# First output-projection tile fed tile by tile, and the second down unit made ready one block earlier

## The reference, cut to what matters

```python
merged = (jax.nn.sigmoid(ga) * (attn_o @ p["w_attn_br"])
          + jax.nn.sigmoid(gr) * (rwkv_o @ p["w_rwkv_br"]))
x = x + gate1[:, None, :] * (merged @ p["w_out"])
h2 = _modulate(_rmsnorm(x, p["norm2_g"]), shift2, scale2)
up = _dwconv3(h2 @ p["ffn_up"], p["ffn_conv"])
up_u, up_g = jnp.split(up, 2, axis=-1)
x = x + gate2[:, None, :] * ((jax.nn.silu(up_g) * up_u) @ p["ffn_down"])
```

## Time and profile before

| what | value |
|---|---|
| median of 3 runs | 1376.88 us (1375.66 to 1378.38) |
| the profiled execution's own time | 1380.84 us |
| its span, first to last instruction | 1379.1 us |
| PE busy in the span | 1294.0 us (94%) |
| DVE busy, ACT busy | 689.9 us (50%), 550.1 us (40%) |
| mean granted TensorE clock | 0.977 |

### The profile page before, as it was taken

One profiled execution on the slowest core, in us unless ns is written; L12 is line 12 of the kernel. 1 busy time (PEld: TensorE's weight loads), 2 busy tenths in 40 slices (PEclk: granted clock), 3 DMA queues, 4 the chain that ended last, 5 costly groups with the idle time before them and its releaser, 6 DMA issues.

```text
span 1379.1 us, 31730 instructions
## 1 busy us (share of the span) xinstructions
PE 1294.0 (94%) x13903; PEld 1196.7 (87%) x13903; DVE 689.9 (50%) x1036; ACT 550.1 (40%) x864; POOL 42.1 (3%) x103
## 2 busy tenths in 40 slices
PE   4899999998999769899999899899999999899996
PEld 1899999997999545499989788799999999899995
DVE  3437642642544676565556412654545545434544
ACT  4645534422233477533342121733334333233433
POOL 0100011000010000010000000000000000000000
PEclk9999999999999998999999999999999999999998
DMA  9322365315000200011017574021221211022222
GB/s 389 143 71 102 110 271 180 105 45 209 8 5 4 92 1 1 0 53 34 8 41 259 225 294 177 31 88 65 64 88 61 91 61 46 23 66 71 69 76 92
DMA packets 24027, 131.70 MB, mean 96 GB/s; under 512 B 2896, under 2 KB 3664, under 8 KB 15344
## 3 DMA queue, kind: packets, MB, share of 16 engines
q1 hardware_dynamic: 19104, 103.98, 21.5%
q0 software_dynamic: 4816, 26.11, 5.0%
HBM read 111.74 MB, written 18.34 MB: 94 GB/s over the span
## 4 chain that ended last, share of the span: by engine, by line
PE 60%; DVE 3%; ACT 2%; issue 1%; DVEq 0%; ACTq 0%
PE ps L712 30%; PE ps L1206 11%; PE ps L882 2%; PE ps L870 2%; PE ps L1093 1%; PE ps L850 1%; PE ps L737 1%; PE ps L756 1%; PE ps L1069 1%; PE ps L999 1%; PE ps L747 1%; DVE nmax L1972 1%; PE ps L1070 1%; PE ps L862 1%; PE ps L1040 1%
## 5 line engine op out<-in xcount | busy, mean ns | idle before, releaser
L712 PE MATMUL ps<-h2lo,whi 128*128 128x322 f32 x672 | 154.5, 311 | 0.7 <-ACT facc L1308 0.7
L712 PE MATMUL ps<-h2hi,wlo 128*128 128x322 f32 x672 | 155.0, 312 | 0.0
L712 PE MATMUL ps<-h2hi,whi 128*128 128x322 f32 x672 | 154.0, 310 | 0.0
L1662 DVE TENSOR_TENSOR wlo<-raw,whi 128x2048 fp32r<-128x2048 f32 x47 | 107.5, 2288 | 70.4 <-ACT whi L1269 70.4
L712 PE MATMUL ps<-hlo,whi 128*128 128x322 f32 x544 | 127.9, 316 | 1.0 <-ACT qkv L1334 1.0
L712 PE MATMUL ps<-hhi,wlo 128*128 128x322 f32 x544 | 125.4, 312 | 0.0
L712 PE MATMUL ps<-hhi,whi 128*128 128x322 f32 x544 | 124.7, 310 | 0.0
L712 PEld LDWEIGHTS ps<-h2hi,whi 128*128 128x128 f32 x672 | 114.2, 190 | 0.0
L712 PEld LDWEIGHTS ps<-h2lo,whi 128*128 128x128 f32 x672 | 113.0, 189 | 0.9 <-DVE wlo L1662 0.9
L712 PEld LDWEIGHTS ps<-h2hi,wlo 128*128 128x128 f32 x672 | 113.6, 189 | 0.0
L1709 DVE SCALAR_TENSOR_TENSOR facc<-fraw,par,facc 128x642 f32<-128x642 f32 x44 | 39.0, 887 | 138.7 <-ACT facc L1308 138.7
(11 more groups left out here) (339 smaller groups left out, 2596.7 us busy)
## 6 DMA issues: line engine op xcount, KB each, us to landing
raw<-in_wblk SPq DMA_DIRECT2D x48, 1024.0 KB, 4.9
adl<-in_wada SPq DMA_DIRECT2D x8, 2048.0 KB, 7.9
raw<-in_wdn SPq DMA_DIRECT2D x44, 256.0 KB, 2.6
adaw<-in_wada SPq DMA_DIRECT2D x4, 2048.0 KB, 20.7
gate_scratch<-gout POOLq DMA_DIRECT2D x16, 322.0 KB, 2.5
gld<-gate_scratch POOLq DMA_DIRECT2D x8, 644.0 KB, 4.6
attention_inputs_used<-attention_scratch SPq DMA_DIRECT2D x1, 5056.0 KB, 15.5
u_scratch<-uout POOLq DMA_DIRECT2D x12, 320.0 KB, 2.4
```

The source lines that it names most:

```text
L712: mm = pe.matmul(o, w, v, start=first, stop=last and w is hi and x is xh[n])
L1662: TT(wlo[s][:, :], raw[s][:, :], whi[s][:, :].bitcast(F32), ALU.subtract).then_inc(lo_done, 1)
```

## The change

The first output tile leaves `dense_block` and becomes `out_first`: it waits for `m_lo` one tile at a time, and `ada_late(4)` moves to just before its last tile. The other seven output tiles stay as they were. For the second down unit, the high and low data go to new tiles laid over the unused part of `raw[0]`, and its weights to columns 512 to 1023 of `whi[0]` and `wlo[0]`; so its ACT part and its DVE part move to between the last two up blocks, behind those of unit 0. ACT's wait for the last `af` tile stays, ahead of the loop over the other units.

```diff
+    spot[0] = raw_at + 4 * 512
+    dhi_second, dlo_second = (sb(name, [P, TP - 2], F32R) for name in ("dhi_second", "dlo_second"))
...
-        pe.wait_ge(tile_evac, 2 * BLK_OUT + 2)
-        ada_late(4)
-        pe.wait_ge(m_lo, KD)
+        def out_first():
+
+            pe.wait_ge(lo_done, BLK_OUT + 1)
+            pe.wait_ge(hi_done, BLK_OUT + 1)
+            pe.wait_ge(tile_evac, 2 * BLK_OUT + 1)
+            for k in range(KD):
+                if k == KD - 1:
+                    pe.wait_ge(tile_evac, 2 * BLK_OUT + 2)
+                    ada_late(4)
+                pe.wait_ge(m_lo, k + 1)
+                hi, lo = (w[BLK_OUT % 2][:, k * 256:k * 256 + P] for w in (whi, wlo))
+                for q, (w, x) in enumerate(((hi, mlo[k]), (lo, mhi[k]), (hi, mhi[k]))):
+                    for o, v in zip(out_halves(0), halves(x)):
+                        mm = pe.matmul(o, w, v, start=k == 0 and q == 0, stop=k == KD - 1 and q == 2)
+            mm.then_inc(tile_done, 1)
...
-        for b in range(BLK_OUT, BLK_UP):
+        out_first()
+        between_out(0)
+        pe.wait_ge(tile_evac, 2 * BLK_OUT + 2)
+        dense_tile(BLK_OUT % 2, 1, range(KD), mhi, mlo, out_halves(2), 256).then_inc(tile_done, 1)
+        between_out(1)
+        for b in range(BLK_OUT + 1, BLK_UP):
...
         def down_unit(n, s, k, again=False):
+
+            second = k == 1 and n == 1
             pe.wait_ge(d_hi, n + 1)
             pe.wait_ge(d_lo, n + 1)
+            xh, xl = (dhi_second, dlo_second) if second else (dhi[s], dlo[s])
             for f in (2, 3, 0, 1) if k == 0 and not again else range(4):
-                hi, lo = whi[s][:, f * P:f * P + P], wlo[s][:, f * P:f * P + P]
+                at = (4 + f if second else f) * P
+                hi, lo = (w[0 if second else s][:, at:at + P] for w in (whi, wlo))
...
-                for q, (w, x) in enumerate(((hi, dlo[s]), (lo, dhi[s]), (hi, dhi[s]))):
+                for q, (w, x) in enumerate(((hi, xl), (lo, xh), (hi, xh))):
...
-            ac.activation(whi[s][:, 0:512], raw[s][:, 0:512], ACT.Copy)
-            ac.activation(dhi[s][:, :], af[:, k, :], ACT.Copy).then_inc(d_hi, 1)
+            second = first and s == 1
+            ac.activation(whi[0][:, 512:1024] if second else whi[s][:, 0:512], raw[s][:, 0:512], ACT.Copy)
+            ac.activation((dhi_second if second else dhi[s])[:, :], af[:, k, :], ACT.Copy).then_inc(d_hi, 1)

         up_block(NBLK - 2, FF - 2, 0, False, False)
-        ac.wait_ge(act_done, 1)
+        ac.wait_ge(act_done, 2)
         ac.wait_ge(tile_done, 2 * NBLK - 2)
         down_hi(0, 0, 0, True)
+        down_hi(1, 1, 1, True)
         up_block(NBLK - 1, FF - 1, 1, False, False)
-
         ac.wait_ge(act_done, FF)
-        ac.wait_ge(tile_done, 2 * NBLK)
-        down_hi(1, 1, 1, True)
...
-        def down_lo(n, s, k):
+        def down_lo(n, s, k, second=False):
             dv.wait_ge(d_hi, n + 1)
-            TT(wlo[s][:, 0:512], raw[s][:, 0:512], whi[s][:, 0:512].bitcast(F32), ALU.subtract)
-            TT(dlo[s][:, :], af[:, k, :], dhi[s][:, :].bitcast(F32), ALU.subtract).then_inc(d_lo, 1)
+            wh, wl = (w[0][:, 512:1024] if second else w[s][:, 0:512] for w in (whi, wlo))
+            xh, xl = (dhi_second, dlo_second) if second else (dhi[s], dlo[s])
+            TT(wl, raw[s][:, 0:512], wh.bitcast(F32), ALU.subtract)
+            TT(xl[:, :], af[:, k, :], xh[:, :].bitcast(F32), ALU.subtract).then_inc(d_lo, 1)

         up_block(NBLK - 2, FF - 2, 0, False)
         down_lo(0, 0, 0)
+        down_lo(1, 1, 1, second=True)
         up_block(NBLK - 1, FF - 1, 1, False)
-        down_lo(1, 1, 1)
```

More of the change, by code:

```diff
@@ L383, in build @@
     yrs = sb("yrs", [P, TP])
+    spot[0] = raw_at + 4 * 512
+    dhi_second, dlo_second = (sb(name, [P, TP - 2], F32R) for name in ("dhi_second", "dlo_second"))
+    assert spot[0] <= raw_at + 4 * WEL
     spot[0] = af_at
```

## The result

The changed kernel takes 1370.68 us (median of 8 runs, 1368.39 to 1372.69); the kernel before, run beside it, 1378.47 (8 runs, 1375.66 to 1383.63). The ratio is 0.9941, with a 95% interval from 0.9926 to 0.9957: by it 8.1 us faster, between 5.9 and 10.2 (the medians differ by 7.8). A second round beside other kernels gave 0.9938 [0.9918, 0.9958]. The forecast was 11.5 us and a time of 1365.4; it had the direction and the two places right, and the size wrong. Part of the distance is the base: the forecast stood on the first three runs of the kernel before, 1376.88.

A forecast was written before the change was run, and what follows sets the result against it. PE was taken as the bound, busy 94% of the span, with idle and half clock at two places. Gains of 5.5 us (output projection) and 6.0 us (down units), 11.5 us off 1376.88, gave 1365.4 us; range 1362.5 to 1370.

The forecast's parts named there:

- Output tile 0 without a pause: At the output projection, PE goes straight on from the branch products; tile 1 starts 5.5 us sooner.
- The wait for tile 6 of `mlo`: In output tile 0, PE waits about 0.3 us for the first of DVE's last two tiles.
- the other new waits: New `m_lo` waits in output tile 0, satisfied on arrival: at most 0.28 us for all seven, taken as nothing.
- (c): Load 6, issued after `ada_late(4)` beside `x`, stalls PE before `ada_late(6)` by 0 to 0.4 us; taken as 0.
- (d): Load of `x`, issue unmoved, has the engines awhile; square of tile 0 needed after `ada_late(6)`, with 0.9 us of cover.
- (e): Loads behind load 6 (load 7, a weight block, load 8) follow `ada_done` and move with PE; no cost booked.
- Rival B: At the first output tiles, `x` lands 3 to 4 us later beside load 6, losing 2 to 3 us: 1368 us, 10%.
- The down units: Units 0 and 1 run in one go and unit 2 ends 6.0 us sooner if the clock stays up.
- Unit 2 behind ACT's wait for the last `af` tile: Before down unit 2, PE still idles 1.9 us, so only 3.4 of the 5.3 us of idle go.
- The clock was booked at its full price: Half clock lost 1.54 us in output tile 0 and 2.68 us in down unit 1; both counted as gained.
- rival A: The clock falls in the 1.9 us stop left before down unit 2, price 2.7 us: 1368.1 us, 10%.
- Rivals C and D: C: one half fails, 1371 us, 4%, both 1376.9, 2%; D: instruction waits in up-block and unit loops, 1385 us, 2%.

The follow-up runs named there:

- e8: The changed kernel with the load of `x` issued 4 us sooner, when the last merge is done: 1370.85 us, ratio 0.9941 to the kernel before.
- e3: The changed kernel with `ada_late(4)` before the fourth merged tile, so load 6 is issued ahead of `x`: 1373.95 us, ratio 0.997 to the kernel before.
- e10: The kernel of e3 with SP holding load 7 and the weight block until `x` is in: 1368.96 us, ratio 0.9933 to the kernel before.
- e2: The changed kernel with the output-tile half undone, only down unit 1 made ready early: ratio 0.9959 to the kernel before, 5.7 us faster.
- e4: The changed kernel without ACT's wait for the last `af` tile ahead of the unit loop: 1368.64 us, ratio 0.993 to the kernel before.
- e5: The kernel before with 36 matmuls on constants between down units 0 and 1: ratio 0.9992, 1.1 us faster.
- e1: The kernel before with only the output-tile half (`out_first`) added, unit 1 made ready late: ratio 0.9985, 2.1 us faster.
- a2: The changed kernel run again without edits, beside other kernels: 1368.71 us, ratio 0.9938 to the kernel before.
- e9: The changed kernel with `x` loaded 4 us sooner and without ACT's wait for the last `af` tile: 1368.05 us, ratio 0.9921 to the kernel before.
- e12: The changed kernel with matmuls on constants, 22 before the up blocks and 12 after down unit 1: 1368.58 us, ratio 0.9922 to the kernel before.
- e13: The kernel before with matmuls on constants: 20 after `ada_late(4)`, 36 after down unit 0, 22 before the up blocks: 1374.61 us, ratio 0.9974.

## Why the prediction was wrong, point by point

- **Output tile 0 without a pause: right.** 5.5 us forecast to tile 1, 5.57 in the trace; from the end of the last branch pair (774.84) to tile 1 it is 13.33 us, forecast 13.3. The wait for tile 6 of `mlo` was 0.3 us as worked out; the other new waits cost nothing visible.
- **The step that failed is (c), "I take 0" for load 6.** Its stop was bounded at 0 to 0.4 us from the slowest landing seen, 12.6 us, and put at 0 from bytes over rate. It was 1.60 us: the load took 13.6 us. Two things are wrong in that sum. It asked only when the last byte of both would land, not which of the two would be served first, though (d) itself gives `x` the engines for a while: `x` had them, and load 6 came 1.6 us after PE was ready for it. And it counted 4.7 MB, `x` and load 6, while (e) let load 7 and the weight block move with PE at no cost. Load 7 moved to 2.95 us behind load 6, and by the time load 6 was in, SP's queue had moved 1.0 MB more than load 6 has; at the 442 GB/s of the prediction that is an estimated 2.2 us of the engines. `e8` shows that `x` close ahead of load 6 is needed for the stop, by taking it away; `e3` shows that load 6 ahead of `x` is worse, and `e10` that load 7 and the weight block were most of that. No run holds load 7 back in the changed kernel, so its share in the 1.60 us stays open. Rival B named this place, with `x` as the late one; it came about for load 6, at half B's price.
- **Who has the engines.** The Trainium skill (DMA: Bandwidth & Descriptors, Queues, rings and completion order) says that each DMA engine takes turns between the queues that have work, a packet at a time. The trace agrees from 789 to 790 us, where the shares are 57.5% and 45.8%. From 784.5 to 788 they are 88.6% and 9.9%. By the rule alone load 6 would have had half of the some 0.4 MB a us that the queues moved in those first 4 us, 0.8 MB, and would have been in an estimated 2 us sooner. The measurement decides; no run here shows what held back its first packets.
- **The down units: right in the trace.** 6.0 us forecast, 5.86 there, and `e2` measured 5.7 (3.4 to 8.0). Unit 2 behind ACT's wait for the last `af` tile, with 1.9 us idle forecast and 1.78 found, was the point on which the half turned from 5.3 us of idle to 3.4, and `e4` confirms it.
- **The clock was booked at its full price, and that was the second error.** 1.5 us at the output projection and 2.7 at the units, both taken from one profiled execution of the kernel before in which the clock fell at both stops, and carried to the median as if any run had them. With the old stop at the output projection it fell in two of three executions (the kernel before and `e5`, not `e2`). The stop of 1.8 us before unit 2 was seen in six (the changed kernel twice, `e2`, `e3`, `e8`, `e10`), and the clock fell in one, `e2`: rival A had 10%, and is what one execution in six does. The long stop of 5.1 us let it fall both times that it was seen unfilled (the kernel before, `e1`). The Trainium skill (TensorE: Matmul & The Clock Gate, What's actually happening) says that the moment at which the clock changes differs from run to run of the same kernel, since what watches PE is not started with the kernel. The traces agree in that equal stops end differently: 1.00 in the changed kernel and 0.54 in `e2` behind 1.78 and 1.79 us, with the same down units.
- **Rivals C and D didn't happen.** Each half did what it says; PE's loads idle for no shown cause 2.1 us in 3 places, as in the earlier trace rows, and the up blocks take 316.9 us up to unit 0 as before.
- **What stays open.** With load 6 and the clock at its seen shares (1.5 us in one of three, 1.5 us in one of six), the sum is 5.5 - 1.6 - 0.5 for the first half and 6.0 - 0.3 for the second, 9.1 us, an estimate; 8.1 and 8.5 were measured, with intervals of some 2 us, so the rest can't be told from nothing. A part of it may lie before the up blocks. There the low clock lasted some 3 us in the profiles of the kernel before, the changed kernel, `e2`, `e3` and `e5`, and 6 to 7 us in those of `a2`, `e1`, `e4`, `e8`, `e9` and `e10`, at a price of 0.5 to 1.2 us up to unit 0. The changed kernel is in both lists (its second profile is `a2`), so the kernel alone doesn't decide it; but all six long ones have the shorter output projection, and whether that makes them likelier was not settled.

## What to carry to other kernels

When a stop is taken out, list what each transfer behind it is issued by and what it is needed by, and count with it what follows it in its queue, since that moves up too. Here `x` well before load 6 took 1.5 us off that stretch of the profile (too little to show in the whole time), and load 6 before `x` made it 1.85 us longer (26.31 against 24.46), mostly through load 7 and the weight block behind it. A wait that stands ahead of a loop holds up the first turn, even if only the last turn needs it (here 1.5 us). A clock that is low after a stop in one profile is a chance, not a price: count it by the share of executions in which it fell, or look at more than one. And compare two profiles from a mark just ahead of the change: here 1.3 of the 10.9 us between the two spans came from before it.

## What the runs showed of the hardware that was not expected

A transfer issued on idle DMA engines moved its first packets within 2 us (load 5 of the kernel before: issued at 776.40, 123 GB/s already from 776 to 778), but one issued 1.8 us behind another queue's 2.6 MB needed 4 us for them, and so did `x` behind load 6 in the kernel before. Matmuls on constants kept PE's clock at 1.00 over a wait of 5 us that otherwise ended at 0.50 (`e5`), yet not in front of the up blocks, where it fell with 0.43 us of idle left (`e12`) and with none (`e13`). Runs of one kernel on this single core spread over 2 us (`e12`) to 10 us (`e10`), 1373.93 to 1382.98 for the kernel before in 23 runs, and the profiles place much of that ahead of the change; so a difference of 2 us stays unclear even after 6 to 12 runs.
